# Input stage of the even layer rebuilt: x in four pieces, other accumulator banks, S5 tables between x chunks, five-product complex matrices, one queue for the kernel matrix

## The reference: what is computed

```
proj = rmsnorm(x) @ w_in                       # 1024 -> 1280: q 512, k 128, v 128, u 512
q, k = rope(rmsnorm(q)), rope(rmsnorm(k))      # banded attention with sinks, window 128
dt  = exp(log_dt); mag = exp(a_re*dt)
lr, li = mag*cos(a_im*dt), mag*sin(a_im*dt)    # per group of 16 channels, 64 complex states
bb  = ((lam - 1)/a) * b                        # complex
s_t = lam*s_{t-1} + bb u_t                     # S5 scan over time, complex
y   = Re(c s) + d*u;  out = gelu(y)*sigmoid(gelu(y) @ w_glu + b_glu)
x   = x + concat(attention, out) @ w_out
```

## Time and profile before

| | us |
|---|---|
| median of 3 runs | 1421.23 |
| runs from, to | 1411.24, 1422.82 |
| the profiled execution | 1418.06 |
| its span in the trace | 1416.3 |
| TensorE busy in the span | 1345.2 (95%) |
| VectorE, ScalarE, POOL busy | 671.9, 433.9, 160.7 |

### The profile page before, as it was taken

How to read it: one execution, slowest core, us unless ns; L and a number is a source line. 1 busy time by engine, 2 the same in 40 slices (tenths; PEclk the granted TensorE clock), 3 DMA queues, 4 the chain that set the end, 5 groups by cost and what they waited for, 6 DMA issues and landing times. The chain is left out here.

```text
span 1416.3 us, 25318 instructions
## 1 busy us (share of the span) xinstructions
PE 1345.2 (95%) x10450; PEld 1286.1 (91%) x10450; DVE 671.9 (47%) x950; ACT 433.9 (31%) x667; POOL 160.7 (11%) x149
## 2 busy tenths in 40 slices
PE   5678889899999999999999999999999999999998
PEld 4667666899999999999988888999999999999998
DVE  3875576564444234444553433367644433344422
ACT  5222355232222112222242444442322221222211
POOL 1573300340000000002300000004200000000000
PEclk9788799999999999999999999999999999999999
DMA  6164211153333322233221211213323332223332
GB/s 170 51 107 74 80 35 31 46 139 90 88 89 102 91 74 86 82 96 103 52 75 46 62 48 47 62 48 103 105 89 89 94 103 71 76 88 89 106 92 75
DMA packets 230634, 115.08 MB, mean 81 GB/s; under 512 B 34533, under 2 KB 226489, under 8 KB 230537
## 3 DMA queue, kind: packets, MB, share of 16 engines
q1 hardware_dynamic: 225912, 113.00, 28.4%
q10 hardware_dynamic: 4656, 1.16, 0.8%
HBM read 107.77 MB, written 7.38 MB: 81 GB/s over the span
## 5 line engine op out<-in xcount | busy, mean ns | idle before, releaser
L315 PE MATMUL ps<-xh,whi 128*128 128x272 f32 x1408 | 291.6, 288 | 2.1 <-DVE wlo L274 2.1
L315 PE MATMUL ps<-xh,wlo 128*128 128x272 f32 x1408 | 291.4, 288 | 0.0
L315 PE MATMUL ps<-xl,whi 128*128 128x272 f32 x1408 | 290.3, 288 | 0.0
L315 PEld LDWEIGHTS ps<-xh,whi 128*128 128x128 f32 x1408 | 221.5, 188 | 2.6 <-issue 2.5
L315 PEld LDWEIGHTS ps<-xl,whi 128*128 128x128 f32 x1408 | 221.2, 188 | 0.0
L315 PEld LDWEIGHTS ps<-xh,wlo 128*128 128x128 f32 x1408 | 219.8, 189 | 0.0
L274 DVE TENSOR_TENSOR wlo<-wraw,whi 128x1024 fp32r<-128x1024 f32 (+1 forms) x118 | 165.2, 1400 | 98.6 <-ACT whi L269 94.2
L269 ACT CAST whi<-wraw 128x1024 fp32r<-128x1024 f32 (+1 forms) x118 | 133.4, 1130 | 140.1 <-PE ps L315 140.1
L315 PE MATMUL ps<-hh,whi 128*128 128x272 f32 x704 | 145.8, 288 | 0.0
L315 PE MATMUL ps<-hl,whi 128*128 128x272 f32 x704 | 145.5, 288 | 0.0
L315 PE MATMUL ps<-hh,wlo 128*128 128x272 f32 x704 | 145.5, 288 | 0.0
(11 more groups left out here) (536 smaller groups left out, 1977.1 us busy)
## 6 DMA issues: line engine op xcount, KB each, us to landing
wraw<-in_w_gate SPq DMA_DIRECT2D x88, 256.0 KB, 3.0
wraw<-in_w_up SPq DMA_DIRECT2D x88, 256.0 KB, 3.1
wraw<-in_w_down SPq DMA_DIRECT2D x32, 384.0 KB, 3.8
wraw<-in_w_in_odd SPq DMA_DIRECT2D x48, 256.0 KB, 3.1
wraw<-in_w_down SPq DMA_DIRECT2D x32, 320.0 KB, 3.2
wraw<-in_w_in_even SPq DMA_DIRECT2D x20, 256.0 KB, 4.5
wraw<-in_w_out_odd SPq DMA_DIRECT2D x16, 256.0 KB, 3.1
ev_xs<-in_x_prompt SPq DMA_DIRECT2D x2, 1024.0 KB, 7.0
```

Of the source, the lines that this page charges most:

```text
L315: ins = pe.matmul(K.ps[:, 2 * s + h, 0:HT], w[s][:, k, :], a[:, k, h * HT:(h + 1) * HT], start=start, stop=stop)
```

## The change

It does ten things, all in `phase_even`:

1. x comes in four pieces of 256 columns instead of two of 512, with the weights of panels 0 and 1 between them. The load of panel 3's weights moves behind the small tables. On ScalarE's queue the gains (`gn`) come ahead of the S5 parameters (`par_in`).
2. Three PSUM places for x chunks instead of two, and panels 0 to 9 use accumulators by `acc_bank`: panels 0, 1, 2 have banks 0, 2, 4; panel 3 takes bank 0 and waits for panel 0, panel 4 takes bank 2 and waits for panel 1.
3. Angles, sines and coefficients come between the x chunks: angles on VectorE at chunk 2, sines on ScalarE after chunk 3, and panel 1's split and the coefficients on VectorE at chunk 5.
4. The transposes of c come in the middle of panel 1, and the token norms' sum in panel 2 (after its sixth chunk) instead of ahead of panel 2.
5. The powers of lam move from VectorE to POOL, ahead of `rot`; POOL no longer waits for `stat`.
6. E by five operations of 2048 elements instead of six, F by five of 1152 for each half instead of six, with sums and differences of the factors prepared (`b_dif`, `b_sum`, `p_sum`, `c_sum`, and `npw` is now a difference).
7. The diagonal matrices by one operation for the prompt and one for the sample, between E's operations; E's operations stand between the evacuations in another order; the swap matrices (`at_swap`) come ahead of `panel_end(3)`.
8. The cosine tables are scaled on ScalarE, behind a wait for F; `rotate(0)` comes ahead of clearing G on POOL.
9. Four of the S5 scan's first products, key norms and rotations in another order around panels 7, 8 and 9, on TensorE, VectorE and ScalarE; `panel(6)` and `panel(7)` are cut in pieces of two chunks between the increments.
10. SP alone sends the local kernel out and fills G.

The diff, cut to its core:

```diff
+    def acc_bank(p):
+        return 2 * (p if p < 3 else (p + 1) % 2 if p < EVEN_OUT else p % 2)
...
-        sp.dma_start(B.xs[:, 0:4, 0:512], x_v[:, :, 0:512]).then_inc(S["x_in"], 16)
+        def quarter(n):
+            sp.dma_start(B.xs[:, 0:4, n * 256:(n + 1) * 256], x_v[:, :, n * 256:(n + 1) * 256]).then_inc(S[f"x_in{n}"], 16)
+        quarter(0)
...
         load(0)
-        sp.dma_start(B.xs[:, 0:4, 512:D], x_v[:, :, 512:D]).then_inc(S["x_in2"], 16)
+        quarter(1)
+        quarter(2)
         load(1)
+        quarter(3)
...
-        kernel_out(sp, range(0, 4))
-        kernel_to_g(sp, range(0, SUB // 2))
+        kernel_out(sp, range(0, 8))
+        kernel_to_g(sp, range(0, SUB))
...
             if k0 == 0:
                 pe.wait_ge(K.lo_ready[s], g.n[s] + i + 1)
-                if i:
-                    pe.wait_ge(K.acc_free[s], g.n[s] + i)
+                if p in (1, 2):
+                    pe.wait_ge(sem("resid_prompt"), DC)
+                    pe.wait_ge(sem("resid_sample"), DC)
+                elif p:
+                    taken(pe, {3: 0, 4: 1, EVEN_OUT: EVEN_OUT - 1, EVEN_OUT + 1: EVEN_OUT - 2}.get(p, p - 2))
...
-        panel(1)
...
+        panel(1, 0, 4)
         pe.wait_ge(S["s5_in"], 96)
...
         ins.then_inc(S["c_t"], 1)
-        panel(2)
+        panel(1, 4)
+        panel(2, 0, 6)
+        pe.wait_ge(S["diag"], 2)
+        pe.wait_ge(S["ct"], 4)
+        for n in range(4):
+            pe.matmul(ps[:, 6, n * P:(n + 1) * P], K.ones[:], B.diag[:, n * P:(n + 1) * P], start=True, stop=True)
+        pe.matmul(ps[:, 7, 0:LS], K.ones[0:LS, :], B.diag[0:LS, LP:T], start=True, stop=True).then_inc(S["bc"], 1)
+        panel(2, 6)
         panel(3)
...
             if k == 0:
-                pe.wait_ge(S["eb"], 6)
+                pe.wait_ge(S["eb"], 5)
                 pe.wait_ge(S["rms"], 2)
-                pe.wait_ge(S["ct"], 4)
+                taken(pe, 2)
...
         panel(8, 0, 1)
         kernel_rows()
-        panel(8, 1, 3)
+        panel(8, 1, 2)
+        pe.wait_ge(S["kn"], 3)
+        head_sums(1)
+        swapped(1)
+        panel(8, 2, 4)
+        pe.wait_ge(S["rs"], 2)
         key_columns()
...
-        split_hi_of(act, 3)
-        act.wait_ge(S["bc"], 1)
...
         act.wait_ge(S["c_t"], 1)
...
+        split_hi_of(act, 3)
+        act.wait_ge(S["bc"], 1)
+        act.copy(K.rstd[:, 0:LP], ps[:, 6, :]).then_inc(S["rms"], 1)
+        act.copy(K.rstd[:, LP:T], ps[:, 7, 0:LS]).then_inc(S["rms"], 1)
...
         split_hi_of(act, 8)
+        act.wait_ge(S["f"], 2)
+        act.wait_ge(S["misc"], 16 * 18)
+        act.activation(B.cos_q[:], cos, ACT.Copy, scale=B.g_qk[:, 0:1]).then_inc(S["cosg"], 1)
+        act.wait_ge(S["cosg"], 2)
+        act.activation(cos, cos, ACT.Copy, scale=B.g_qk[:, 1:2]).then_inc(S["cosg"], 1)
         act.wait_ge(S["bz"], 2)
...
-        kernel_out(act, range(4, 8))
-        kernel_to_g(act, range(SUB // 2, SUB))
...
+            if m == 2:
+                angles()
+            if m == 5:
+                split_lo_of(dve, 1)
+                coefficients()
         low(DC - 1)
...
+        dve.wait_ge(S["powers"], 1)
+        dve.tensor_tensor(ev[0], pb[2], bv[0], ALU.mult).then_inc(se, 1)
+        dve.tensor_tensor(ev[1], pb[0], bv[1], ALU.mult).then_inc(se, 1)
+        dve.wait_ge(S["sinv"], 2)
+        dve.wait_ge(S["const"], 16)
+        dve.tensor_tensor(B.diag[:, 0:LP].rearrange("p (n c) -> p n c", n=4), K.ident.unsqueeze(1).broadcast_to([P, 4, P]),
+                          B.stat[:, 0:4].unsqueeze(2).broadcast_to([P, 4, P]), ALU.mult).then_inc(S["diag"], 1)
+        dve.tensor_scalar(B.diag[0:LS, LP:T], K.ident[0:LS, 0:LS], B.stat[0:LS, 4:5], None, ALU.mult).then_inc(S["diag"], 1)
         dve.wait_ge(se, 2)
+        dve.tensor_tensor(ev[1], ev[1], ev[0], ALU.add).then_inc(se, 1)
+        split_lo_of(dve, 3)
+        evac(0)
+        evac(1)
+        split_lo_of(dve, 4)
+        dve.tensor_tensor(B.e_tmp[:], pb[1], bv[2], ALU.mult).then_inc(se, 1)
+        dve.wait_ge(se, 4)
+        evac(2)
         dve.tensor_tensor(ev[0], ev[0], B.e_tmp[:], ALU.subtract).then_inc(se, 1)
...
-        pool.wait_ge(S["stat"], 5)
+        pool.wait_ge(S["lam"], 2)
+        st(pool.memset(pw[0][:, :, 0:1], 1.0), sr)
...
+            cmul(st, pool, sr, pw[0][:, :, n + 1:2 * n + 1], pw[1][:, :, n + 1:2 * n + 1], *a, *wb, B.rot_tmp[:, :, 0:n])
+        st(pool.tensor_tensor(B.p_sum[:], pw[0][:], pw[1][:], ALU.add), sr)
+        st(pool.tensor_tensor(npw[:], pw[0][:], pw[1][:], ALU.subtract), sr)
...
-        pool.wait_ge(S["eb"], 6)
         pool.wait_ge(S["ct"], 4)
+        pool.tensor_tensor(B.c_sum[:], ct[0][:], ct[1][:], ALU.add).then_inc(S["cosg"], 1)
+        pool.wait_ge(S["eb"], 5)
...
+            st(pool.tensor_tensor(f[0], cs, p0, ALU.mult), sr)
+            st(pool.tensor_tensor(f[1], c0, pd, ALU.mult), sr)
+            st(pool.tensor_tensor(t, c1, ps_, ALU.mult), sr)
             st.sync()
-            st(pool.tensor_tensor(f[0], f[0], t, ALU.subtract), sr)
+            st(pool.tensor_tensor(f[1], f[1], f[0], ALU.subtract), sr)
             st.sync()
...
+            pool.tensor_tensor(f[0], f[0], t, ALU.subtract).then_inc(S["f"], 1)
...
```

More of the change, by code:

```diff
@@ L570, in even_buffers @@
     B.band, B.identr = tails[5]("at_band", [P, 2 * P], F32R), tails[5]("at_identr", [P, P], F32R)
+    tails = [Region(nc, K.panels_at + n * FH * P * 4 + DC * P * 4) for n in range(6)]
+    B.c_sum, B.p_sum = tails[0]("s5_c_sum", [P, NPAIR, S5H]), tails[2]("s5_p_sum", [P, NPAIR, SUB + 1])
+    B.b_dif, B.b_sum = (tails[n](f"s5_b_{m}", [P, NPAIR, S5H]) for n, m in ((1, "dif"), (3, "sum")))
     B.sq = Region(nc, 16512 + -(-K.places["head_back"][0] * 4 // 64) * 64)("at_sq", [P, T])
@@ L695, in _ @@
                          allow_slow_non_contiguous=True).then_inc(S["misc"], 16)
+        load(3)
         for m in range(4):
@@ L900, in _ @@
         increments(0)
-        panel(6, 2, 5)
+        panel(6, 2, 4)
         increments(1)
-        panel(6, 5)
+        panel(6, 4, 6)
         increments(2)
+        panel(6, 6)
+        increments(3)
         panel(7, 0, 2)
-        increments(3)
-        panel(7, 2, 5)
         increments(4)
-        panel(7, 5)
+        panel(7, 2, 4)
         increments(5)
+        panel(7, 4)
         key_rows()
@@ L1133, in _ @@
                     .then_inc(S["gn_in"], 16)
[L1134 to L1135 removed]
+        for n, x in enumerate(("s5_a_re", "s5_a_im", "s5_log_dt")):
+            act.dma_start(B.par_in[16 * n:16 * n + 16, :], I[x][0].rearrange("(j two) p -> j (two p)", two=2)).then_inc(S["par_in"], 16)
         act.wait_ge(S["gn_t"], 1)
[L1137 to L1142 removed]
+        act.copy(K.gains[:].rearrange("p n c -> p (n c)"), ps[:, 1, 0:4 * DC]).then_inc(S["gains"], 1)
         act.wait_ge(S["gains"], 1)
@@ L1150, in _ @@
             act.wait_ge(S["x_t"], m + 1)
-            act.copy(K.resid[:, m, 0:LP], ps[:, 4 + 2 * (m % 2), :]).then_inc(sem("resid_prompt"), 1)
-            if m < 2:
-                split_hi_of(act, m)
-            if m:
-                high(m - 1)
-        high(DC - 1)
+            act.copy(K.resid[:, m, 0:LP], ps[:, (4, 6, 2)[m % 3], :]).then_inc(sem("resid_prompt"), 1)
+            if m == 0:
+                split_hi_of(act, 0)
+            high(m)
+            if m == 0:
+                act.wait_ge(S["small"], 1)
+                act.activation(sm("dt"), B.par[:, 32:48], ACT.Exp).then_inc(S["act"], 1)
+            if m == 1:
+                act.wait_ge(S["small"], 3)
+                act.activation(sm("mag"), sm("ard"), ACT.Exp).then_inc(S["act"], 1)
+            if m == 3:
+                act.wait_ge(S["small"], 12)
+                act.activation(sm("wi"), sm("r"), ACT.Sin).then_inc(S["act"], 1)
+                act.activation(sm("wr"), sm("carg"), ACT.Sin).then_inc(S["act"], 1)
+            if m == 4:
+                split_hi_of(act, 1)
         def square(n):
@@ L1431, in _ @@
[L1431 to L1439 removed]
+            dve.tensor_copy(K.resid[:, m, LP:T], ps[:, 1 + (4, 6, 2)[m % 3], 0:LS]).then_inc(sem("resid_sample"), 1)
@@ new lines, in _ @@
+        dve.wait_ge(S["tab"], 32)
+        dve.wait_ge(S["misc"], 16 * 18)
+        for x in range(2):
+            dve.tensor_scalar(B.sw[x][:], swap, B.g_qk[:, 1 - x:2 - x], None, ALU.mult).then_inc(S["swg"], 1)
+        dve.tensor_scalar(B.nsink[:], B.nsink[:], -1.0, None, ALU.mult).then_inc(S["ns"], 1)
+        dve.tensor_scalar(B.nsink_s[:], B.nsink_s[:], -1.0, None, ALU.mult).then_inc(S["ns"], 1)
+        dve.tensor_scalar(B.b_glu[:], B.b_glu[:], 0.5, None, ALU.mult).then_inc(S["ns"], 1)
@@ L1533, in _ @@
             .then_inc(S["idd"], 1)
+        sr, t = S["r"], B.tp[:]
+        dve.wait_ge(S["xsb"], 12)
+        dve.wait_ge(S["rot"], 1)
+        st(dve.tensor_tensor(R[0][:], X[0][:], rot[0][:], ALU.mult), sr)
+        st(dve.tensor_tensor(t, X[1][:], rot[1][:], ALU.mult), sr)
+        st(dve.tensor_tensor(R[1][:], X[1][:], rot[0][:], ALU.mult), sr)
+        st.sync()
```

(2 more changed lines are left out.)

274 lines of the change are left out of this document (110 added, 164 removed).

## The result

The changed kernel took 1396.12 us, the median of 4 runs (1392.28 to 1398.90); the kernel before, timed beside it, 1416.91 (4 runs, 1411.24 to 1422.82). The ratio is 0.984, with a 95% interval of 0.981 to 0.987. The profiled execution took 1395.11 us with a span of 1392.9; before it was 1418.06 and 1416.3. The forecast was 1399, its range 1383 to 1411.

What follows compares the result with a forecast made beforehand. The stage from 31.6 to 166.3 us was taken as bound by a small-table chain through VectorE, POOL and ScalarE. 1418 - 20 gave 1398, or 1401 on the median's level; forecast 1399 us, range 1383 to 1411.

Steps and rivals of the forecast that it cites:

- Front, 0 us: Stage to 31.6 us: earlier TensorE start offset by table steps between x chunks; 0, bounds 2 us less or more.
- POOL's powers at 39.5: Powers of lam on POOL, following its 8th power, ready at 39.5 us; bounds 35.5 and 42.
- E at 64.5: E's first transposes after the powers at 64.5 us instead of 77.5, 13 us earlier; bounds 59 and 68.
- POOL becomes the bound: Table stage: `rot` ends at 74.6 behind E, F at 101, only 7.6 us earlier, and ScalarE waits for F.
- Scaled keys at 115: Scaled key rows, after the last increment at 107, come at 115 us instead of 124.4.
- From the keys' end to `outputs(0)`, 31 us: Stretch from scaled keys to `outputs(0)`: 31 us instead of 42, with ScalarE's DMA issuing and late squares gone.
- `outputs(0)` at 146, -20 us: End of the second stage: `outputs(0)` starts at 146 us, 20 us earlier than before.
- G hidden by 6 us: SP alone sends the local kernel and fills G; G there at about 140, 6 us before needed.
- A: Rival: POOL is light, small operations cost VectorE nothing; powers 35.5, E 59, `outputs(0)` 135, 1387 us; chance 0.22.
- B: Rival: POOL a full lock against VectorE from 20 us; F 111, `outputs(0)` 156, 1408 us; 0.22 together with D.
- C: Rival: slower, POOL's operations at 3.12 us throughout plus the full lock; F 125 gives 1424 or more; chance 0.06.
- D: Rival: no effect, E earlier but a wait for G or ScalarE fills the place; 0.22 together with B.

Runs made afterwards that it cites:

- halves: Changed kernel with x in two pieces of 512 columns again instead of four quarters: median 1395.96 us, ratio 0.986 to the kernel before.
- the shared F: Changed kernel with the second half of F computed on VectorE, POOL doing the first alone: median 1391.06 us, ratio 0.982 to the kernel before.
- the version above: Changed kernel with F split between POOL and VectorE, VectorE's scan products and ScalarE's increments reordered: 1383.80 us, ratio 0.977 to the kernel before.
- the longer F: Changed kernel with one product of F done twice in each half on POOL, twelve operations instead of ten: median 1401.70 us, ratio 0.988.
- swap matrices late: Changed kernel with swap matrices and three small scalings behind panel 5's evacuation again: median 1397.09 us, ratio 0.984 to the kernel before.

## Why the prediction was right, step by step

- **Front, 0 us:** panel 0 ended 2.1 us earlier (panel 1 began at 31.61, now at 29.51), just past the bound of 2. The x pieces alone gave nothing at the end, as halves showed.
- **POOL's powers at 39.5:** 36.1. The 8th power ended at 25.3 instead of 28 (it began at 18.62 and took 6.7 us, not 8), and the powers took 10.8 us instead of 11.5. This was mis-sized, and the next links inherit it.
- **E at 64.5:** 60.09. From the powers it took 24.0 us instead of 25.0. VectorE waited 2.69 us for POOL, as said.
- **Increments at 85.5, "late next is u":** 81.25, behind a wait for u of 4.20. From E 21.2 us, forecast 21.
- **`rot` 74.6, F 101, "POOL becomes the bound":** 71.13 and 97.6. The durations were right: `rot` 35.0 us (22.5 + 12.5), F 25.5 (25.8). The bound is shown by the longer and the shared F. What I left out is that E's chain is only 5 to 6 us shorter.
- **TensorE's wait of 6.6 us for the last increment:** 5.29.
- **Scaled keys at 115:** the forecast is of the end of the key rows (124.4 before), which is now at 111.4: 3.6 early. F's end gives 3.4 of it; from there to the last increment it took 4.4 us, as forecast.
- **From the keys' end to `outputs(0)`, 31 us:** 32.5, where it was 41.9. The size is nearly right, the reason failed. I put what went to the DMAs that leave ScalarE; they are worth 2.7 us at `outputs(0)`, the order of the scan, the key norms and the rotations 3.5. By the rows above, 5.1 of the 9.4 us are products at a higher granted clock, which the working does not price. TensorE stood idle for 5.8 us, where the working has waits of 2 to 3. What I missed is the 4.33 us wait at 138.59: the third query rotation stands behind the scan's last products on VectorE, POOL's sum behind that rotation, and ScalarE's square behind POOL. In the version above, with the products moved forward, this wait is 2.1.
- **`outputs(0)` at 146, -20 us:** 143.93, -22.4. The keys' 3.6 us and the stretch's 1.5 have opposite signs, so the sum is nearer than the first of them; that is luck.
- **Sum, 1399:** 1396.1. The forecast stood on a kernel before of 1418 to 1421 us. Timed beside the change it took 1416.9, from which my 20 us give 1397; the medians differ by 20.8.
- **G hidden by 6 us:** issued by 128.8, 6.9 us to land, so there near 136; 8 us of cover.
- **Behind `outputs(0)` no change:** 92.8 and 1156.2 us, 1.0 us less together.

Of the rivals, A's first half came (powers 36.1, E 60.1) and its second did not: small POOL operations do pay. B, the full lock with no gap used, would have put F at 111; it ended at 97.6, as VectorE was idle from 47.0 to 52.6 and from 78 to 91 us and POOL worked there. The Trainium skill (SBUF — State Buffer, "Who interferes with whom") states that a VectorE operation with two SBUF inputs and a GpSimd operation that reads SBUF exclude each other, and that the later one is blocked for the whole of the earlier one. The alternating rows of the shared F agree. Scalings with one input waited as well (`s_b_glu_t`, 2.58 us), of which that statement says nothing. C and D did not come. The working names the lower clock level but never prices it: 9.3 us of the gain is the same products run more often at the higher one.

## What to carry to other kernels

When work moves to an idle engine, follow what it delays there up to the next wait of the engine that matters: moving the powers back cost 7.4 us of the end, with them on POOL F was the next bound, and splitting F between both engines gained 5.2. Undo each part alone before giving it credit: of the five that were undone here, two gave nothing at the end (x in pieces, early swap matrices). The other three and the longer F add up to 17.4 of the 22.4 us at `outputs(0)`. E by five operations, the accumulators, the diagonal matrices, the cosines on ScalarE and the panels in pieces were undone in no run, so what each of them is worth stays open; nor need parts that were undone one at a time add up. Where a wait goes, look at once for what ends last behind it, as the swap matrix's wait turned into one for u.

## What the runs showed of the hardware

A VectorE scaling of 128x4 took 0.16 us where it fell between two of POOL's operations of `rot` (61.45 in the changed kernel), and 2.58 us where it met one of F's (swap matrices late: 79.70 to 82.28, POOL's from 79.63 to 82.26). POOL's operations on 16 columns took 2.34 and 3.55 us beside E's operations, against 0.22 to 0.25 for their like; the longer one spans the rest of E's sum and the `wlo` behind it. This fits a small operation waiting for the end of the other engine's large one, whichever of the two engines it is on.
